# A fused two-block kernel: the end of a gated convolution, four up products and two gate sums rearranged

## The chip, the cores and the metric

One Trainium2 chip, one core of it. The metric is the device time of one execution in microseconds (us), the median of the runs. The engines are named as in the profile: PE is TensorE, PEld its weight load, DVE VectorE, ACT ScalarE, POOL GpSimd, SP SyncE.

## The reference, cut to what matters

The first block has two layers. In each, three branches (attention, pooling, neighbourhood attention) are projected, gated and summed, then an output product, and then a gated MLP with a short convolution:

```python
z = jnp.einsum('bsnc,ncd->bsnd', ys, w_branch[l])
gates = jax.nn.sigmoid(gl + b_gate[l]).reshape(B, S, N_BRANCH, D_MODEL)
merged = jnp.sum(gates * z, axis=2)
mix = jnp.einsum('bsd,de->bse', merged, w_out[l])
```

The second block begins with a gated convolution over 31 positions, with a layer norm, and an output product with a bias:

```python
u = h @ w_in + b_in
u = u[..., :D_MODEL] * jax.nn.sigmoid(u[..., D_MODEL:])
u = causal_dwconv(u, dw, dw_b)
u = layer_norm(u, ln_g, ln_b)
u = jax.nn.silu(u)
return u @ w_out + b_out
```

It then has two more gated MLPs and a dilated attention. There are 512 tokens and 1024 channels, all in float32.

## The kernel before, in words

**Products.** A weight product takes three TensorE passes over numbers split into a high and a low part (`whi`, `wlo`, and `hh`, `hl` or `yh`, `yl` or `uh`, `ul`). Weights come in chunks of 1 MB that SP loads into two slots `wraw` in a fixed order; `hi` on ACT (L817) makes `whi`, `lo` on DVE (L1278) makes `wlo`. `lo(c)` makes the low part of chunk c + 2, once PE is done with chunk c, and the load of chunk c waits until the low part of chunk c - 2 is made. PE accumulates in eight banks of 128 x 512 (`bank(0)` to `bank(7)`). All engines run programs written out in order, with semaphores between them.

**Up products (`ffn`, four of them).** `first_two` computes the first two chunks into banks 0 and 4, 1 and 5. Then a loop takes two chunks in a turn; the first goes to banks 2 and 3, the second to 0 and 1. Before each, PE waits for `conv_done`, the count of tiles that DVE has read out (L1476). In the first turn the first of these waits is for banks 0 and 4, which this chunk doesn't write.

**Gates and branches (`merge`, two layers, three branches).** For each branch n and half g there are two gate chunks (`gate_rows`, banks 6, 7 and 4, 5) and one branch chunk (`branch_rows`, banks 0 to 3). DVE adds the gate bias (L1725), ACT takes the sigmoid (L1138), DVE multiplies by the branch (L1732) and adds to `mg` (L1735), which a memset (L1718) clears first. Banks 4 and 5 are held by the attention and the pooling until the end of both, so PE waits for them (`y_lo`, `pool_lo`) ahead of the second gate chunk. At that point POOL starts `weight_sums`: four copies and four additions of 2.5 MB in DRAM, for later down products.

**End of the gated convolution.** The 31 taps of a channel tile are shared: DVE does `DVE_TAPS[t]` of them one after the other (L1798), PE the rest as 32 x 32 products (`partial_taps`, L2445), ACT copies the partial sums out, PE joins them (L2453), and DVE adds the two (L1773). For the last tile that is 11 taps on DVE and 20 on PE. Then the mean is taken by products with `meanm` (L2480, L2483), DVE subtracts it (L1848), ACT squares (L1198), and PE adds the squares up in products one column wide (L2491); POOL adds four tiles of squares into one (L691) so that PE takes five instead of eight. `keep_warm` (L1994) is a product of 512 columns whose result nobody reads. ACT takes the root, PE spreads it (L2495), DVE scales (L1859), ACT applies SiLU and splits, DVE makes the low part (L1284).

**Output product and hand-over.** `out_product` fills banks 4 to 7 (first half of the channels), then `last_two` banks 0 to 3. `hand_over` normalises, adds to the stream, and turns the rows for the next product. Only in the one after the gated convolution (h == 4) DVE first adds the bias `b_out` to each bank (L1325, L1336), and ACT waits for that before it squares.

Of the kernel before, what the change touches and what calls it, by code (L numbers as in the profile page):

```python
# [21 lines left out]
ALU = mybir.AluOpType  # L22
# [17 lines left out]
DVE_TAPS = (15, 15, 15, 15, 15, 15, 15, 11)  # L40
# [129 lines left out]
def build(nc, A, out):  # L170
    with ExitStack() as ctx:
# [67 lines left out]
        with ExitStack() as s:  # L239
# [3 lines left out]
            tapd = [sb(f"tapd{i}", 20 * 32, stack=s) for i in range(2)]  # L243
            part, usum, stack = sb("part", 8 * T, stack=s), sb("usum", T, stack=s), sb("stack", 32, stack=s)
# [9 lines left out]
        def bank(b, n=1):  # L254
# [18 lines left out]
        squared, summed, rooted, diagonal, spread, sq_added = (  # L273
            sem(n) for n in ("squared", "summed", "rooted", "diagonal", "spread", "sq_added"))
        gains_in, biased, half_squared, half_meaned, rest_squared, post_rooted = (
            sem(n) for n in ("gains_in", "biased", "half_squared", "half_meaned", "rest_squared", "post_rooted"))
# [360 lines left out]
        def _(pool):  # L637
# [46 lines left out]
            def add_squares():  # L684

                n = None
                for t in range(3, KT - 2):
                    pool.wait_ge(squared, t + 1)
                    if n:
                        ch.wait(n)  # L690
                    ins = gp.tensor_tensor(tile(sq, 2), tile(sq, 2), tile(sq, t), ALU.add)  # L691
                    if t < KT - 3:
                        n = ch.mark(ins)
                ins.then_inc(sq_added, 1)

# [78 lines left out]
            pool.dma_start(stack[:, :], A["c_stack"]).then_inc(stack_in, 16)  # L774
            pool.wait_ge(stack_in, 16)
# [11 lines left out]
            add_squares()  # L787
            pool.wait_ge(ln_scaled, KT)
            const(ub[:, 0:D], bass.AP(tensor=A["cm_b_out_2"].tensor, ap=[[0, P], [1, D]], offset=A["cm_b_out_2"].offset))
# [16 lines left out]
        def _(act):  # L806
# [45 lines left out]
            def half_squares(h, c, rows=(0, 1, 2, 3)):  # L852

                for b in rows:
                    if h == 4:
                        act.wait_ge(biased, b + 1)
                    elif h % 2:
# [9 lines left out]
            def post_root(h, c, b):  # L867

                if h == 4:
                    act.wait_ge(biased, 4 + b + 1)  # L870
                else:
                    act.wait_ge(*row_done(h, c, b))
# [194 lines left out]
            for l in range(2):  # L1067
# [78 lines left out]
                for g in range(2):  # L1146
                    for j in range(2):
                        gate(2, g, j)
                        if g == 1 and j == 0:
                            for t in range(4):  # L1150
                                act.wait_ge(merged, 9 * l + 5)
# [1488 lines left out]
```

## Time and profile before

| | |
|---|---|
| median of 3 runs | 3115.69 us (3114.3 to 3117.58) |
| the profiled execution's own time | 3114.26 us |
| its span, first to last instruction | 3112.5 us |
| PE busy | 98% |
| DVE, ACT, POOL busy | 59%, 41%, 6% |
| mean granted TensorE clock | 0.995 of 2.4 GHz |

Times of events are us from the start of the span. A number in brackets behind a row of the timeline is how long the engine was idle before it, and who ended that.

### The profile page before, as it was taken

How to read it: one execution, taken by the hardware profiler on the slowest of the kernel's cores; microseconds unless marked ns; L12 is line 12 of the kernel's file. 1: busy time of each engine (PE TensorE's matmuls, PEld its weight loads, DVE VectorE, ACT ScalarE, POOL GpSimd, SP SyncE). 2: the span in 40 equal slices, each digit the busy share in tenths (PEclk: the TensorE clock that was granted, in tenths of full speed). 3: DMA queues.
4: the chain of work that ended last, by engine and by line, in shares of the span. 5: the costliest groups of instructions: out<-in, count | busy, mean ns of one | idle time of the engine just before them, and what ended most of it. 6: DMA issues, size and time to landing. Idle time of an engine off the chain costs nothing.

```text
span 3112.5 us, 42337 instructions
## 1 busy us (share of the span) xinstructions
PE 3059.4 (98%) x16887; PEld 2530.3 (81%) x16887; DVE 1824.1 (59%) x2476; ACT 1263.0 (41%) x1786; POOL 178.9 (6%) x230
## 2 busy tenths in 40 slices
PE   7999999999999999999999989999999999999999
PEld 7767888888887688888888668888888988988887
DVE  4574446557755744556678866557743433465576
ACT  3563234335544622433464343336531221343355
POOL 2030000000012100000001110000000000000000
PEclk9999999999999999999999989999999999999999
DMA  6206853224532288322353157987432323233244
GB/s 174 71 28 220 193 141 108 95 94 143 167 89 79 74 238 199 98 95 95 106 183 97 54 186 182 302 192 210 144 110 95 109 88 102 95 110 100 94 133 158
DMA packets 298730, 408.95 MB, mean 131 GB/s; under 512 B 19796, under 2 KB 211324, under 8 KB 298332
## 3 DMA queue, kind: packets, MB, share of 16 engines
q1 hardware_dynamic: 251036, 306.75, 30.4%
q0 software_dynamic: 47552, 100.21, 13.6%
q8 instruction: 102, 1.67, 0.2%
q14 instruction: 40, 0.33, 0.0%
HBM read 400.54 MB, written 90.18 MB: 158 GB/s over the span
## 4 chain that ended last, share of the span: by engine, by line
PE 86%; DVE 8%; ACT 2%; DMA 1%; issue 1%; DVEq 0%; ACTq 0%; SPq 0%; POOL 0%; POOLq 0%
PE ps L1964 19%; PE ps L1966 19%; PE ps L1965 19%; PE ps L2119 4%; PE ps L2120 4%; PE ps L2121 4%; PE ps L2071 2%; PE ps L2073 2%; PE ps L2072 2%; PE ps L2524 1%; PE ps L2525 1%; PE ps L2526 1%; DVE t_wlo L1278 1%; DMA t_wraw<-in_w_in_dram 1%; DVE t_vb L1798 1%
## 5 line engine op out<-in xcount | busy, mean ns | idle before, releaser
L1964 PE MATMUL ps<-t_hh,t_whi 128*128 128x512 f32 (+1 forms) x2720 | 1015.0, 373 | 12.2 <-DVE t_accv L1476 5.1
L1966 PE MATMUL ps<-t_hh,t_wlo 128*128 128x512 f32 (+1 forms) x2720 | 1005.1, 370 | 0.0
L1965 PE MATMUL ps<-t_hl,t_whi 128*128 128x512 f32 (+1 forms) x2720 | 1004.9, 369 | 0.0
L1278 DVE TENSOR_TENSOR t_wlo<-t_wraw,t_whi 128x2048 fp32r<-128x2048 f32 x198 | 455.7, 2302 | 778.9 <-ACT t_whi L817 778.8
L817 ACT ACTIVATE t_whi<-t_wraw 128x2048 fp32r<-128x2048 f32 x198 | 379.3, 1916 | 1056.7 <-PE ps L1966 848.8
L1964 PEld LDWEIGHTS ps<-t_hh,t_whi 128*128 128x128 f32 x2720 | 513.3, 189 | 114.9 <-issue 16.8
L1965 PEld LDWEIGHTS ps<-t_hl,t_whi 128*128 128x128 f32 x2720 | 513.5, 189 | 87.0 <-issue 2.4
L1966 PEld LDWEIGHTS ps<-t_hh,t_wlo 128*128 128x128 f32 x2720 | 513.4, 189 | 86.8
L2119 PE MATMUL ps<-t_whi,t_ah 128*128 128x512 f32 x528 | 206.0, 390 | 0.0
L2121 PE MATMUL ps<-t_whi,t_al 128*128 128x512 f32 x528 | 205.4, 389 | 0.0
L2120 PE MATMUL ps<-t_wlo,t_ah 128*128 128x512 f32 x528 | 205.4, 389 | 0.0
L1295 DVE TENSOR_TENSOR t_wlo<-t_wraw,t_whi 128x1024 fp32r<-128x1024 f32 x148 | 181.1, 1224 | 19.7 <-ACT t_whi L842 19.1
L842 ACT ACTIVATE t_whi<-t_wraw 128x1024 fp32r<-128x1024 f32 x148 | 155.0, 1047 | 11.3 <-PE ps L2121 5.1
L840 ACT ACTIVATE t_ah<-t_mid 128x512 fp32r<-128x512 f32 x132 | 82.7, 626 | 118.9 <-PE ps L2121 105.4
L1293 DVE TENSOR_TENSOR t_al<-t_mid,t_ah 128x512 fp32r<-128x512 f32 x132 | 91.0, 689 | 67.0 <-ACT t_ah L840 67.0
L1476 DVE SCALAR_TENSOR_TENSOR t_accg<-ps,t_pvec,t_accg 128x511 f32<-128x511 f32 (+1 forms) x176 | 119.5, 742 | 0.0
L1476 DVE SCALAR_TENSOR_TENSOR t_accv<-ps,t_pvec,t_accv 128x511 f32<-128x511 f32 (+1 forms) x176 | 119.4, 742 | 0.0
L2119 PEld LDWEIGHTS ps<-t_whi,t_ah 128*128 128x128 f32 x528 | 99.1, 188 | 21.6 <-issue 1.2
L2121 PEld LDWEIGHTS ps<-t_whi,t_al 128*128 128x128 f32 x528 | 99.1, 188 | 20.5
L2120 PEld LDWEIGHTS ps<-t_wlo,t_ah 128*128 128x128 f32 x528 | 99.1, 188 | 20.3
L2524 PE MATMUL ps<-t_whi,t_hh 128*128 128x256 f32 x384 | 110.2, 287 | 0.0
L2526 PE MATMUL ps<-t_whi,t_hl 128*128 128x256 f32 x384 | 108.6, 283 | 0.0
(320 smaller groups left out, 4097.8 us busy)
## 6 DMA issues: line engine op xcount, KB each, us to landing
t_wraw<-in_w_in_dram SPq DMA_DIRECT2D x46, 1024.0 KB, 5.6
t_wraw<-in_w_up_dram SPq DMA_DIRECT2D x44, 1024.0 KB, 5.0
t_wraw<-in_ffn_w_in_dram SPq DMA_DIRECT2D x44, 1024.0 KB, 5.6
t_wraw<-sum_T SPq DMA_DIRECT2D x80, 512.0 KB, 4.0
sum_T<-in_w_down_dram POOLq DMA_DIRECT2D x12, 2560.0 KB, 32.1
sum_T<-in_ffn_w_out_dram POOLq DMA_DIRECT2D x12, 2560.0 KB, 30.6
t_wraw<-in_w_kv_dram SPq DMA_DIRECT2D x24, 1024.0 KB, 5.1
sum_T<-sum_T POOLq DMA_DIRECT2D x8, 2560.0 KB, 19.9
```

Source lines behind the costliest of these rows:

```text
L817: sc.activation(whi[slot][:, :], wraw[slot][:, :], ACT.Copy).then_inc(w_hi, 1)
L842: sc.activation(whi[slot][:, c0:c0 + 2 * T], wraw[slot][:, c0:c0 + 2 * T], ACT.Copy).then_inc(p_hi, 1)
L1278: v.tensor_tensor(wlo[slot][:, :], wraw[slot][:, :], whi[slot][:, :].bitcast(F32), ALU.subtract).then_inc(w_lo, 1)
L1295: v.tensor_tensor(wlo[slot][:, c0:c0 + 2 * T], wraw[slot][:, c0:c0 + 2 * T], whi[slot][:, c0:c0 + 2 * T].bitcast(F32), ALU.subtract).then_ ...
L1476: ins = v.scalar_tensor_tensor(out=tile(acc, m)[:, o0:o1], in0=from_bank(s, m)[:, i0:i1], scalar=col(cw, r), in1=tile(acc, m)[:, o0:o1], o ...
L1964: te.matmul(out, wh, xh, start=first, stop=False)
L1965: te.matmul(out, wh, xl, start=False, stop=False)
L1966: return te.matmul(out, wl, xh, start=False, stop=last)
L2119: te.matmul(o, lh, wh, start=opens and k == 0, stop=False, skip_group_check=n >= 20)
L2120: te.matmul(o, lh, wl, start=False, stop=False, skip_group_check=n >= 20)
L2121: ins = te.matmul(o, ll, wh, start=False, stop=closes and k == 1, skip_group_check=n >= 20)
L2524: te.matmul(o, xh, wh, start=k == 0, stop=False)
```

## The change

- `DVE_TAPS[7]` goes from 11 to 7, so PE does 24 taps of the last tile.
- POOL no longer adds squares; PE takes all eight tiles of them. All `keep_warm` products go.
- The bias `b_out` is loaded early into a buffer of its own (`brow`), and PE puts it into the eight banks of the output product itself, as `ident` times `brow`, an accumulation that the product then goes on with (`bias_in`, `opened`). Two banks are filled behind the mean, two behind the squares, three behind the spread, and the last between the two chunks of the first half. DVE's eight additions and ACT's waits for them go.
- The second `lo` of this stage, `lo(c + 7)`, moves from behind the centring into the scaling, behind its sixth tile.
- In `ffn` the third and fourth chunk are written out ahead of the loop; the third waits for its weights alone.
- In `merge` the second gate chunk of the first branch goes to banks 0 and 1 and ahead of the wait for `y_lo`; its branch chunk takes tiles 2 and 3 first, and waits ahead of tile 0 until DVE has read the gate. The first branch's product is written straight into `mg`, so the memset and one addition per half go; DVE's loop over two branches is written out.

```diff
-DVE_TAPS = (15, 15, 15, 15, 15, 15, 15, 11)
+DVE_TAPS = (15, 15, 15, 15, 15, 15, 15, 7)
...
+            const(brow[:, :], bass.AP(tensor=A["cm_b_out_2"].tensor, ap=[[0, P], [1, D]], offset=A["cm_b_out_2"].offset))
...
-            add_squares()
             pool.wait_ge(ln_scaled, KT)
-            const(ub[:, 0:D], ...)
...
-                if h == 4:
-                    dve.wait_ge(tables, 16 * 9)
-                    dve.wait_ge(w_used, c + 1)
-                    for b in range(4):
-                        v.tensor_tensor(bank(4 + b), bank(4 + b), ub[:, 0:T], ALU.add).then_inc(biased, 1)
...
-                cleared = ch.mark(v.memset(mg[:, :], 0.0))
...
+                    out = gates[:, :] if n else tile(mg, 4 * g, 4)
+                    v.tensor_tensor(out, gates[:, :], bank(0, 4), ALU.mult).then_inc(drained, 1)
...
-            lo(c + 7)
...
+                if t == 5:
+                    lo(c + 7)
...
+            def bias_in(*banks):
+
+                for b in banks:
+                    te.matmul(bank(b), ident, brow[:, 0:T] if b >= 4 else brow[:, T:D], start=True, stop=False)
...
                 first_two(c, f"pre{2 * f + 1}")
-                with pe.Fori(1, FT // 2) as i:
+                pe.wait_ge(w_lo, c + 3)
+                rows_out(c, (hh, hl), bank0=2).then_inc(w_used, 1)
+                pe.wait_ge(w_lo, c + 4)
+                pe.wait_ge(conv_done, 4 + 2 * m0 + 4)
+                rows_out(c + 1, (hh, hl), bank0=0).then_inc(w_used, 1)
+                with pe.Fori(2, FT // 2) as i:
...
+                    for t in tiles:
+                        if t == 0 and tiles[0]:
+                            pe.wait_ge(drained, 2 + d + 2)
...
+                gate_rows(0, 0, 1, 0)
                 pe.wait_ge(y_lo, PAIRS[f"A{l}"] + 4)
+                branch_rows(0, 0, (2, 3, 0, 1))
                 pe.wait_ge(pool_lo, 4 * l + 4)
-                gate_rows(0, 0, 1)
-                branch_rows(0, 0)
...
-            for t in (0, 1, KT - 2, KT - 1, 2):
-                if t in (KT - 2, 2):
-                    keep_warm()
-                pe.wait_ge(*((sq_added, 1) if t == 2 else (squared, t + 1)))
+            pe.wait_ge(tables, 16 * 9)
+            bias_in(5, 1)
+            for t in range(KT):
+                pe.wait_ge(squared, t + 1)
...
-            keep_warm(1)
+            bias_in(4, 0)
             pe.wait_ge(diagonal, 1)
             te.matmul(bank(3), meanm, std, start=True, stop=True).then_inc(spread, 1)
-            keep_warm(2)
+            pe.wait_ge(centred, KT)
+            pe.wait_ge(rooted, 1)
+            bias_in(7, 2, 6)
             pe.wait_ge(drained, 2 + d + 8)
-            pe.wait_ge(h_lo, SPLIT["ln"] + 1)
-            out_product(2, (uh, ul), "ln", None)
+
+            def last_bias():
+
+                pe.wait_ge(ln_scaled, KT)
+                bias_in(3)
+
+            out_product(2, (uh, ul), "ln", None, last_bias)
```

## Rows read from the trace of the kernel before

**Rows 1.** The page, busy time of each engine and its share of the span.

```profile
PE 3059.4 (98%) x16887; PEld 2530.3 (81%) x16887; DVE 1824.1 (59%) x2476; ACT 1263.0 (41%) x1786; POOL 178.9 (6%) x230
```

**Rows 2.** The waits, of PE: us in total, times, longest.

```profile
PE ps L1964 <- DVE t_accv L1476: 5.1, 4, 1.3
PE ps L2483 <- DVE t_small L1777: 3.7, 2, 3.3
...
PE ps L1964 <- DVE t_yl L1453: 2.8, 2, 1.4
```

**Rows 3.** The timeline of DVE, the last taps: start, us, instruction.

```profile
1786.58 12.00 DVE L1798 SCALAR_TENSOR_TENSOR t_vb<-t_ub,t_pvec,t_vb 128x512 f32<-128x512 f32 x18
1798.50 0.68 DVE L1773 TENSOR_TENSOR t_vb<-t_vb,ps 128x512 f32<-128x512 f32 x1
1799.22 0.75 DVE L1798 SCALAR_TENSOR_TENSOR t_vb<-t_ub,t_pvec,t_vb 128x512 f32<-128x512 f32 x1
...
1800.00 0.69 DVE L1773 TENSOR_TENSOR t_vb<-t_vb,ps 128x512 f32<-128x512 f32 x1
```

**Rows 4.** The timeline of PE, from the mean to the output product (two passes per product).

```profile
1799.36 1.12 PE L2483 MATMUL ps<-t_vb,t_base 128*128 128x512 f32 x2 [3.28 <-DVE t_small L1777]
1800.87 2.08 PE L2483 MATMUL ps<-t_vb,t_base 128*128 128x512 f32 x2 [0.39 <-DVE t_small L1777]
1804.39 3.57 PE L2491 MATMUL ps<-t_base,t_sq 128*128 128x1 f32 x16 [1.44 <-ACT t_sq L1198]
...
1816.35 2.05 PE L1994 MATMUL ps<-t_base 128*128 128x512 f32 x2
1818.20 1.92 PE L2495 MATMUL ps<-t_gain,t_base 128*128 128x512 f32 x2
1819.91 2.52 PE L1994 MATMUL ps<-t_base 128*128 128x512 f32 x4
1823.22 0.47 PE L2071 MATMUL ps<-t_whi,t_uh 128*128 128x512 f32 x1 [0.80 <-DVE t_ul L1284]
```

**Rows 5.** Windows there: us; busy PE, PEld, DVE, ACT, POOL; PEclk; DMA share; GB/s.

```profile
1797.28:1800.69 3.41, 1.12 (x2) 0.30 (x2) 3.33 (x6) 0.00 (x0) 0.00 (x0) 1.00 0.00 0
...
1807.52:1810.93 3.41, 3.41 (x12) 2.38 (x11) 3.41 (x2) 1.00 (x2) 3.16 (x2) 0.50 0.00 0
...
1817.76:1821.17 3.41, 3.41 (x5) 1.58 (x5) 1.17 (x3) 0.63 (x2) 0.00 (x0) 0.50 0.28 109
```

**Rows 6.** Windows from the output product to the third up chunk: first layer, gated convolution.

```profile
441.62:513.70 72.08, 70.51 (x418) 62.47 (x416) 45.07 (x60) 33.54 (x55) 1.14 (x2) 1.00 0.29 93
...
1823.22:1903.68 80.46, 73.92 (x417) 65.11 (x417) 48.30 (x66) 37.93 (x63) 7.89 (x8) 0.96 0.74 231
```

**Rows 7.** The timeline of PE, products two columns wide at full clock, layer 0.

```profile
149.83 1.84 PE L2313 MATMUL ps<-t_base,t_gain 128*128 128x2 f32 x16
```

**Rows 8.** Groups of DVE from 1847 to 1880: busy, mean ns, idle before.

```profile
L1278 DVE TENSOR_TENSOR t_wlo<-t_wraw,t_whi 128x2048 fp32r<-128x2048 f32 x3 | 6.9, 2292 | 9.0 <-ACT t_whi L817 9.0
...
L1336 DVE TENSOR_TENSOR ps<-ps,t_ub 128x512 f32<-128x512 f32 x4 | 2.8, 690 | 0.0
```

**Rows 9.** Windows of PE in the first MLP: us, PE busy (x), PEclk, DMA share, GB/s.

```profile
514.00:604.00 90.00, 90.00 (x398) 1.00 0.30 100
```

**Rows 10.** The timeline at the first gates of layer 0: PE, then DVE, SP and ACT.

```profile
255.26 0.50 PE L1964 MATMUL ps<-t_hh,t_whi 128*128 128x512 f32 x1 [1.42 <-DVE t_yl L1453]
...
270.71 1.40 DVE L1725 TENSOR_SCALAR t_gates<-ps,t_pvec 128x512 f32<-128x512 f32 x2
...
261.80 0.37 SPq L570 DMA_DIRECT2D t_wraw<-in_w_in_dram  x1
...
282.04 1.92 ACT L817 ACTIVATE t_whi<-t_wraw 128x2048 fp32r<-128x2048 f32 x1 [8.83 <-DMA t_wraw<-in_w_in_dram]
```

**Rows 11.** The timeline of PE at the third up chunk of the first MLP.

```profile
512.14 0.28 PE L1966 MATMUL ps<-t_hh,t_wlo 128*128 128x256 f32 x1
513.70 0.50 PE L1964 MATMUL ps<-t_hh,t_whi 128*128 128x512 f32 x1 [1.28 <-DVE t_accv L1476]
```

More of the change, by code:

```diff
@@ L242, in build @@
             ub, vb = sb("ub", KT * UW, stack=s), sb("vb", KT * T, stack=s)
-            tapd = [sb(f"tapd{i}", 20 * 32, stack=s) for i in range(2)]
-            part, usum, stack = sb("part", 8 * T, stack=s), sb("usum", T, stack=s), sb("stack", 32, stack=s)
+            tapd = [sb(f"tapd{i}", 24 * 32, stack=s) for i in range(2)]
+            part, usum, stack, brow = (sb(n, w, stack=s) for n, w in (("part", 8 * T), ("usum", T), ("stack", 32), ("brow", D)))
         with ExitStack() as s:
@@ L272, in build @@
         init_in, init_turn, init_out, stored = sem("init_in"), sem("init_turn"), sem("init_out"), sem("stored")
[L273 to L276, printed above, removed]
+        squared, summed, rooted, diagonal, spread = (
+            sem(n) for n in ("squared", "summed", "rooted", "diagonal", "spread"))
+        gains_in, half_squared, half_meaned, rest_squared, post_rooted = (
+            sem(n) for n in ("gains_in", "half_squared", "half_meaned", "rest_squared", "post_rooted"))
         x_new, row_squared, pre_rooted, rows_ready, rows_turned = (
@@ L682, in by_tile @@
                 return ap.rearrange("p i n -> i p n")
[L684 to L694, printed above, removed]
             for l in range(2):
@@ L1722, in gate @@
                 def gate(n, g, j, l=l, c=c):
[L1723 removed]
+                    lo(c + 6 * n + 3 * g + j)
+                    b0 = 0 if (n, g, j) == (0, 0, 1) else 6 - 2 * j
                     for m in range(2):
[L1725 to L1726 removed]
+                        ins = v.tensor_scalar(tile(gates, 2 * j + m), bank(b0 + m),
+                                              col("b_gate", 8 * n + 24 * l + 4 * g + 2 * j + m), None, ALU.add)
                     ins.then_inc(drained, 1)
                 def weighted_sum(n, g, l=l, c=c, d=d):
[L1730 to L1738 removed]
+                    lo(c + 6 * n + 3 * g + 2)
+                    dve.wait_ge(gate_sig, 12 * l + 4 * n + 2 * g + 2)
+                    out = gates[:, :] if n else tile(mg, 4 * g, 4)
+                    v.tensor_tensor(out, gates[:, :], bank(0, 4), ALU.mult).then_inc(drained, 1)
+                    dve.wait_ge(drained, 2 + d + 6 * n + 3 * g + 3)
+                    if n:
+                        v.tensor_tensor(tile(mg, 4 * g, 4), tile(mg, 4 * g, 4), gates[:, :], ALU.add).then_inc(merged, 1)
+                        dve.wait_ge(merged, 7 * l + 2 * n + g - 1)
+                for n in range(2):
                     for g in range(2):
@@ L1989, in rows_out @@
                 return row_tile(c, bufs, 1, bank(b0 + 1))
-            def keep_warm(n=1):
-                for _ in range(n):
-                    te.matmul(bank(5), meanm, base[:, 0:T], start=True, stop=True)
+            def bias_in(*banks):
+                for b in banks:
+                    te.matmul(bank(b), ident, brow[:, 0:T] if b >= 4 else brow[:, T:D], start=True, stop=False)
             def turn_row(name, b, turned_in=None):
@@ L2063, in first_two, with token_tile @@
                 rows_half(c + 1, (hh, hl), 1, 1).then_inc(w_used, 1)
-            def token_tile(c, bufs, b, half, k0, k1, last, ks=None):
+            def token_tile(c, bufs, b, half, k0, k1, last, ks=None, opened=False):
                 for k in (ks or range(k0, k1)):
@@ L2070, in token_tile @@
                     o = bank(4 * (1 - half) + b)
-                    te.matmul(o, xh, wh, start=k == 0, stop=False)
+                    te.matmul(o, xh, wh, start=k == 0 and not opened, stop=False)
                     te.matmul(o, xh, wl, start=False, stop=False)
@@ L2074, in token_tile, with tokens_mix @@
                 return ins
-            def tokens_mix(c, half, bufs, k0, k1, last, ready=None):
+            def tokens_mix(c, half, bufs, k0, k1, last, ready=None, opened=False):
                 pe.wait_ge(w_lo, c + 1)
```

58 lines of the change are left out of this document (16 added, 42 removed).

## The prediction

> **What bounds the kernel now.** First the page: PE is busy for 98% of the span [rows 1], so a part of the change can only pay where PE stands idle, runs at the lower clock, or does less. Then the waits of PE [rows 2]: three of them lie where the change works. PE waits four times, 5.1 us in all, for the readout of the first up tiles; twice, 2.8 us, for the last low part of the attention; and twice, 3.7 us, for DVE's last taps. Then, for the end of the convolution, the timelines of DVE and PE and windows with the granted clock [rows 3 to 5]. The reader is to see a chain: DVE's taps end late, PE idles for 3.28 us, the clock falls to 0.50 at 1800.69, and it is back only at 1821.17, although PE is busy in each window between. What fills those windows is mostly products one column wide. So this stretch costs twice, by idle time and by the clock. Last, windows from the first product of an output product to the third up chunk: 72.08 us in the first layer, 80.46 behind the convolution [rows 6].
>
> **The last taps.** From 1786.58 to 1798.50 DVE does 18 taps, two tiles in alternation, 0.66 us each; one behind another of the same tile takes 0.78 (1799.22 to 1800.00) [rows 3]. Four taps fewer: three of the 18 and the one at 1799.22. Two of those left, and the addition, now stand behind their own tile, 3 x 0.12 more. Before the first addition: 11.92 - 3 x 0.66 + 0.36 = 10.3, so it starts at 1796.9; the second addition follows at once, and the signal that PE got at 1800.87 [rows 4] comes at 1798.45, 2.4 us earlier. PE takes 16 products of 32 x 32 more; no row here prices them, but PE idled 3.28 us just behind [rows 4], so a cost up to that is covered; I take about 1 us. The idle shrinks to about 1 us.
>
> **The mean.** A product of 512 columns took 1.12 us with its tail at the full clock and 2.08 at the half [rows 4]. With PE nearly always busy I take the clock as full here. The centring, which started 0.1 us behind 1800.87 + 2.08, then starts at 1799.8, 3.2 earlier.
>
> **Squares and first biases.** One product of 512 columns holds PE for 1.71 us at the half clock (1818.20 to 1819.91), so 0.86 at the full. `bias_in(5, 1)` is 1.7 us, 1799.5 to 1801.2, and lies beside the 1.40 us that centring and squaring take (1.44 of idle at 1804.39). It delays nothing. Each tile of squares is eight passes: 3.57/16 = 0.22 us a pass with the tail, so 1.7 us a tile at the half clock; at the full clock the two-column products took 1.70/16 = 0.11 a pass [rows 7], 0.87 a tile. Eight tiles: 7.0 us at full, 13.7 at half. Before, five tiles and two `keep_warm` and the wait for POOL took 1804.39 to 1816.35 = 12.0. Which clock? In the window 1807.52:1810.93 PE was busy throughout, more than half of it with a full-width product, and the clock stayed at 0.50 [rows 5]; so I take it to fall while the squares run, at 1805 as a middle. By then 4.4 tiles are done; 3.6 at 1.71 end at 1811.2, and the root comes at 1811.5 against 1816.5. The Trainium skill, TensorE: Matmul & The Clock Gate, Part 1, says that an idle PE brings the lower clock and sustained activity the full one. Read plainly, a PE without a gap would keep 2.4 GHz; the row just named doesn't bear that out. That reading is rival A.
>
> **Spread and the other biases.** `bias_in(4, 0)` is queued ahead of the spread: 3.4 us at the half clock, while the diagonal needed 1.7 (1816.5 to 1818.2). So the spread waits 1.7 to 2 us for the biases; at the full clock (1.7) it waits for nothing. Spread ends and DVE scales at 1811.4 + 3.4 + 1.95 = 1816.7 against 1820.15 (3.4 earlier). `bias_in(7, 2, 6)` is 2.6 to 5.1 us beside the 2.9 us to the first low part (1820.15 to 1823.07); the products of full width in a row raise the clock again, as they did at 1821.17, so I take it as covered. The output product starts at 1819.6 instead of 1823.2: **3.6 us**. Bounds: full clock throughout gives 1814.3 (8.9); the clock down already at the mean gives 1826.2 (minus 3.0), with 13.7 for squares, 3.7 and 3.4 and 5.1 for biases in line.
>
> **The moved `lo`.** It puts one low part, 2.3 us [rows 8], into DVE's scaling, behind tile 6 of 8. PE takes 10.9 us for the first chunk (48 products of 90/398 = 0.226) [rows 9], then needs this low part at about 13.9 us behind the start of scaling; it is there at 9.2 (six scalings and four low parts of 0.69, then 2.3). The tiles behind it are needed one per 2.7 us from 13.9 on and come from 10.7 on: covered by 3 us or more. Behind it in SP's queue is the load of the fourth output chunk, issued at 1826 instead of 1814, and behind the eighth scaled tile POOL starts its 10 MB of copies, at 1828. The load is needed on chip by about 1842.6. In layer 0 a load amid such copies took 261.80 to 282.04 = 20.2 us [rows 10]; so the bound is 1846, some 3 us late; with a head start of 3 us I take nothing. POOL itself loses three additions and one load.
>
> **The hand-over.** Eight additions of 0.69 us on DVE go (four at L1336, as many at L1325), 5.5 us [rows 8], and ACT's waits for them. The first layer has the same stage without them: 80.46 - 72.08 = 8.4 us, of which PE idle is 6.54 - 1.57 = 5.0 and the clock (0.96 against 1.00) the rest [rows 6]. Added: `bias_in(3)`, in line, 0.9. Sum **7.5 us**. Bounds: 3.5 if up weights loaded amid POOL's copies come late (in this stage the DMA share is 0.74 against 0.29), 8.4 if the bias were free.
>
> **Third up chunk.** Its weights are ready ahead of it. The gap is 513.70 - 512.14 - 0.12 (half of 0.226 and a little, for a product of 256 columns) = 1.44 us [rows 11], and DVE had all of this turn's reads done 4 us before the fourth chunk wants them. Four times: **5.8 us**; bounds 5.1 [rows 2] and nothing, if a later wait took it back; no other wait of PE in these loops is in the list.
>
> **Gates.** PE no longer idles at 255.26: 1.42 and a short start, 1.6. The branch chunk then runs two tiles, 24 x 0.226 = 5.4 us, but the gate is read 272.1 - 266.1 = 6.0 us behind the chunk's end [rows 10], so a new wait of 0.6: net 1.0 for each layer. Dropped DVE work (memset 3.5, four additions of 2.3) hides beside PE and gains nothing itself, but lets the next load start 1.7 us earlier. Behind, in layer 0, PE meets a chunk that came late from DRAM (the wait ended at 282.04); if its landing doesn't move, that layer gains nothing. **2.0 us**; bounds 0.5 and 3.
>
> **The sum.** 3.6 + 7.5 + 5.8 + 2.0 = 18.9. Against the execution's own time, 3114.26 (span 3112.5 and 1.8 around it): 3095.4. The median of the runs is 1.4 above that execution: **3096.8**.
>
> **The rivals.** A, the squares hold the full clock: the tail gives 8.9, the time is 3091.5. For it: PE has no long gap left. Against: [rows 5]. B, the clock is already down at the mean: the tail loses 3.0, 3103.4. For it: joins with small gaps stand ahead of it. Against: before the 3.28 us gap it held at 1.00. C, the hand-over waits for up weights behind POOL's copies, which now stand nearer to it: 4 us less, 3100.8. For it: 20.2 us a load. E, the bank moves don't do what they say, since the next wait on DVE or DRAM takes their place: 7.8 less, 3104.6. D, slower: the fourth output chunk, now issued only 2 us ahead of POOL's copies, lands with them instead of in 20 us. DVE's part, and PE, hand-over and all, wait for it. From a landing at 1842.6 + 18.9 = 1861.5 on, the kernel is slower than before; landing after 50 us, 1876, gives 33 lost, 3130. Against it: each load seen amid copies came in about 20. The Trainium skill, DMA: Bandwidth & Descriptors, Queues, rings and completion order, says that an engine takes turns between queues packet by packet; by it a load shares, and is not held to the end of the copies, which agrees with 20.2 us and keeps D small.
>
> **How the numbers follow.** Forecast 0.50; A 0.14; B 0.12; C 0.12; E 0.08; D 0.04. What is left of a fixed difference is told from none from 0.2%, 6.2 us, on. A to E alone all lie beyond it, but B, C and E together would give 3112: I leave 0.04 for such a sum, taken from theirs. So faster 0.92, same 0.04, slower 0.04. The range goes from 3091 (A) to 3105 (E).
>
> **What would show it.** The signal behind the last tap near 1798.4, and no idle of PE over 1.5 us ahead of the mean; one fall of the clock during the squares and none in the hand-over; first output product near 1819.6 and 71.5 us from there to the third up chunk; no wait for L1476 at the up products; at the gates a wait for L1725 of 0.6 in place of 1.4. Wrong would be: a DMA as the one who ends a wait of L817 in the hand-over, or the biases in line for over 6 us.

## The result, and the profile after

The changed kernel takes 3096.47 us (median of 4 runs, 3095.39 to 3098.06), the kernel before on the same chip 3114.99 (4 runs, 3112.68 to 3117.58). The ratio is 0.9941 with a 95% interval of 0.9929 to 0.9952: 18.5 us faster, against 18.9 forecast. The profiled execution has a span of 3095.0 us and took 3096.8 us.

Below, the page of after, busy time by engine, against [rows 1]. PE still is the bound; it is busy as long as before, and idles less.

```profile
PE 3058.1 (99%) x16949; PEld 2529.8 (82%) x16949; DVE 1799.1 (58%) x2458; ACT 1263.1 (41%) x1786; POOL 173.4 (6%) x227
```

The waits of PE after, against [rows 2]: us in total, times, longest. Four waits for the readout (`t_accv`) are one, 3.7 us for the last taps (`t_small`) are 0.8, and a gate's wait (`t_gates`) is new in place of the one for `t_yl`.

```profile
PE ps L1933 <- DVE t_accv L1444: 1.3, 1, 1.3
...
PE ps L1933 <- DVE t_gates L1693: 0.9, 3, 0.4
PE ps L2459 <- DVE t_small L1746: 0.8, 1, 0.8
```

The end of the convolution after, timelines of DVE (against [rows 3]) and of PE (against [rows 4]): start, us, instruction, idle before.

```profile
1782.20 10.26 DVE L1767 SCALAR_TENSOR_TENSOR t_vb<-t_ub,t_pvec,t_vb 128x512 f32<-128x512 f32 x15
1792.50 0.69 DVE L1742 TENSOR_TENSOR t_vb<-t_vb,ps 128x512 f32<-128x512 f32 x1
...
1794.05 0.06 DVE L1746 MEMSET t_small<- 128x1 f32 x1
```

```profile
1793.37 1.98 PE L2459 MATMUL ps<-t_vb,t_base 128*128 128x512 f32 x4 [0.84 <-DVE t_small L1746]
1795.19 1.88 PE L1963 MATMUL ps<-t_brow,t_base 128*128 128x512 f32 x4
1796.91 9.29 PE L2467 MATMUL ps<-t_base,t_sq 128*128 128x1 f32 x64
1806.05 3.76 PE L1963 MATMUL ps<-t_brow,t_base 128*128 128x512 f32 x4
1809.61 1.92 PE L2471 MATMUL ps<-t_gain,t_base 128*128 128x512 f32 x2
1811.31 3.05 PE L1963 MATMUL ps<-t_brow,t_base 128*128 128x512 f32 x6
```

PE now works without a gap from the mean to the output product (1814.63, behind 0.27 us of idle), and the mean's product is at full clock. Windows of after: us; busy PE, PEld, DVE, ACT, POOL; PEclk; DMA share; GB/s. The first runs from the mean over `bias_in(5, 1)` into the squares, at full clock; the second is the rest of the squares, at half; the third is `bias_in(4, 0)`. The last is the stage from the output product to the third up chunk (which starts at 1886.29), against [rows 6].

```profile
1794.00:1801.60 7.60, 7.60 (x51) 5.92 (x50) 6.27 (x10) 4.82 (x8) 0.00 (x0) 1.00 0.01 3
1801.70:1806.00 4.30, 4.30 (x22) 4.30 (x22) 0.76 (x1) 0.00 (x0) 0.00 (x0) 0.50 0.54 154
1806.06:1809.60 3.54, 3.54 (x5) 1.48 (x6) 1.05 (x5) 1.55 (x2) 0.00 (x0) 0.50 0.26 102
...
1814.63:1886.43 71.80, 71.50 (x419) 63.13 (x420) 43.84 (x58) 36.63 (x62) 7.37 (x7) 1.00 0.79 253
```

The clock falls once, at 1801.69 in the squares, and is full again from 1811.93 on.

**Where the 17.5 us of span came from.** Positions of the same product in both traces give: gates of layer 0 1.5; third up chunk of the first MLP 1.5; gates of layer 1 0.5; second MLP 1.6; tail of the convolution 3.9; hand-over behind it 7.4; third MLP 0.0; fourth MLP 1.5. That is 17.9, less 0.5 by which this execution began later. The same code was profiled a second time ("The changed kernel again", below), and there the same positions give 21.5 (parts and sum are rounded alone):

| | forecast | after | after, second profile |
|---|---|---|---|
| tail | 3.6 | 3.9 | 5.4 |
| hand-over | 7.5 | 7.4 | 7.3 |
| third up chunk, four times | 5.8 | 4.6 | 6.0 |
| gates, two layers | 2.0 | 2.0 | 2.8 |
| sum | 18.9 | 17.9 | 21.5 |

So a part read from one profile can be off by 1.5 us.

The third MLP's zero is the place of the first profile that differs most from the forecast. Its third chunk has no wait any more, but four chunks on PE waits 1.28 us. Timelines of POOL, SP, ACT and PE there: an addition between DRAM tensors is under way from 1900.49 to 1930.83; the load of up weights issued at 1905.24 beside it lands 19.1 us later; ACT, which had waited for it for 8.53 us, splits it late, and PE stops. PE's wait names the readout, which stands behind that split in ACT's queue.

```profile
1900.49 1.92 POOL L674 DMA_DIRECT2D sum_T<-in_ffn_w_out_dram  x1 [25.79 <-issue]
1905.24 0.37 SPq L570 DMA_DIRECT2D t_wraw<-in_ffn_w_in_dram  x1
1924.35 1.92 ACT L804 ACTIVATE t_whi<-t_wraw 128x2048 fp32r<-128x2048 f32 x1 [8.53 <-DMA t_wraw<-in_ffn_w_in_dram]
1931.28 0.50 PE L1933 MATMUL ps<-t_hh,t_whi 128*128 128x512 f32 x1 [1.28 <-DVE t_accv L1444]
```

### The profile page after: what moved, and what is told of

Same layout as the page of the kernel before. It is cut to its first block, busy times and chain, and to the rows that moved or that the text cites. A ratio compares the mean times of both kernels' runs of the same rounds, so it can differ in the third digit from the quotient of the medians.

```text
span 3095.0 us, 42330 instructions
## 1 busy us (share of the span) xinstructions
PE 3058.1 (99%) x16949; PEld 2529.8 (82%) x16949; DVE 1799.1 (58%) x2458; ACT 1263.1 (41%) x1786; POOL 173.4 (6%) x227
## 4 chain that ended last, share of the span: by engine, by line
PE 85%; DVE 8%; DMA 4%; ACT 2%; issue 1%; DVEq 0%; ACTq 0%; SPq 0%; POOL 0%; POOLq 0%
PE ps L1933 18%; PE ps L1935 18%; PE ps L1934 18%; PE ps L2088 4%; PE ps L2090 4%; PE ps L2089 4%; DMA t_wraw<-in_w_in_dram 3%; PE ps L2040 2%; PE ps L2042 2%; PE ps L2041 2%; DVE t_wlo L1260 1%; PE ps L2507 1%; PE ps L2508 1%; PE ps L2509 1%; ACT t_whi L804 1%; PE ps L2149 1%
## 5 line engine op out<-in xcount | busy, mean ns | idle before, releaser
L804 ACT ACTIVATE t_whi<-t_wraw 128x2048 fp32r<-128x2048 f32 x198 | 379.3, 1916 | 1053.5 <-PE ps L1935 834.9
L2089 PEld LDWEIGHTS ps<-t_wlo,t_ah 128*128 128x128 f32 x528 | 99.1, 188 | 20.5
L2508 PE MATMUL ps<-t_wlo,t_hh 128*128 128x256 f32 x384 | 108.6, 283 | 0.0
```

Source lines behind the costliest of these rows:

```text
L804: sc.activation(whi[slot][:, :], wraw[slot][:, :], ACT.Copy).then_inc(w_hi, 1)
L2089: te.matmul(o, lh, wl, start=False, stop=False, skip_group_check=n >= 20)
```

## Experiments

Two theories of the gain stand against each other. Mine: four parts with a price each (tail 3.6, hand-over 7.5, third up chunk 5.8, gates 2.0), independent of one another. The rival: PE waits taken out are given back at the next late load, so that parts don't add up. Every ratio is to the kernel before on the same chip. Three distances read from each trace do most of the work, in us:

| kernel | A: second MLP's first up product to output product | B: from there to the 73rd up product behind the last turned rows | C: the next 912 up products |
|---|---|---|---|
| before | 519.48 | 73.27 | 203.22 |
| after | 513.99 | 65.90 | 203.21 |
| after, second profile | 512.62 | 65.94 | 201.81 |
| up products only | 517.88 | 73.27 | 203.75 |
| gates only | 518.07 | 73.27 | 203.44 |
| bias by DVE | 513.72 | 75.87 | 202.75 |
| 11 taps | 515.69 | 65.92 | 202.01 |
| biases between squares | 515.95 | 65.97 | 203.43 |
| wide squares | 510.52 | 67.53 | 203.98 |
| wide, filled | 510.52 | 65.93 | 206.17 |
| POOL's squares | 514.05 | 65.93 | 204.03 |
| sums early | 518.69 | 65.90 | 201.63 |
| sums beside the down products | 543.70 | 65.92 | 201.63 |
| sums spread | 510.54 | 75.61 | 201.63 |

A holds the second MLP's third chunk (1.5 of the 519.48 - 517.88 = 1.6 is that part) and the tail. Its spread between executions is as large: 1.4 between the two profiles of after, and 1.4 between before and the kernel with the gates only, whose edit touches nothing in A; in both pairs the clock's low stretch in the tail differs. C without any wait is 201.63; what is above it is waits, with up to 0.3 us behind each in which PE is slower than its usual pace. One profile stands behind each row.

**The up products alone.** The kernel before, with

```diff
-                with pe.Fori(1, FT // 2) as i:
+                pe.wait_ge(w_lo, c + 3)
+                rows_out(c, (hh, hl), bank0=2).then_inc(w_used, 1)
+                pe.wait_ge(w_lo, c + 4)
+                pe.wait_ge(conv_done, 4 + 2 * m0 + 4)
+                rows_out(c + 1, (hh, hl), bank0=0).then_inc(w_used, 1)
+                with pe.Fori(2, FT // 2) as i:
```

> The kernel before, with only the third and fourth chunk of the four up projections written out and the third put into the banks that need no drain. By the prediction's step for the up products (four waits of 1.28 to 1.45 us removed) it is 5.8 us faster than before. The rival is what the changed kernel's trace shows at its third up projection: there the gain of 1.44 us was lost again, to a wait of 1.28 us that ends with a late load of up weights. If that wait is the price of the earlier hand-over (GpSimd's copies between DRAM tensors then lie nearer the loop), it is absent here and all four places give 1.4 us; if it is the price of the earlier third chunk alone, it is here too, and the sum is 4.4 us.

Measured: 3109.99 against 3114.55, ratio 0.9986 (0.9977 to 0.9995), 4.6 us faster. The four waits are gone, and in the third MLP two came in their place (0.38 us, and the row below); its C is 203.75 against 203.22. So the third MLP gave nothing here either, with the hand-over unmoved: the earlier hand-over isn't needed for the late load. By positions the other three places gave 1.5 each and the third MLP -0.5, 4.1 us in all; the rest of this profile's 4.8 is chance at the gates and the tail. The runs' interval (1.6 to 7.2 us) holds 5.8 as well as 4.4, so it is the trace, of one execution, that speaks for the second theory.

```profile
2052.74 0.50 PE L1964 MATMUL ps<-t_hh,t_whi 128*128 128x512 f32 x1 [1.13 <-DVE t_accv L1476]
```

**The gates alone.** The kernel before, with the gates' part of the diff.

> The kernel before, with only the gates' part: the second gate chunk to banks 0 and 1, the branch product's tiles in the order 2, 3, 0, 1, and the first branch stored in place of cleared and added. The prediction gave 1.0 us a layer, 2.0 in all. The trace of the changed kernel reads 1.5 us in the first layer and 0.5 us in the second, which is the same sum: if the two parts are independent of the rest, this kernel reads 2.0 us faster than before. If later loads take the gain back once the up products don't use it, it reads 0 to 1 us.

Measured: 3112.99 against 3114.55, ratio 0.9995 (0.9986 to 1.0004), 1.6 us, which by itself isn't told from nothing. The trace shows both halves of the step. The wait of 1.42 us is gone and one of 0.36 is there, as in after; and later in layer 0 stands a wait of 1.09 for a chunk that came late, where the kernel before had 0.44 and 0.29, after 0.30, and the second profile of after nothing.

```profile
271.14 0.50 PE L1965 MATMUL ps<-t_yh,t_whi 128*128 128x512 f32 x1 [0.36 <-DVE t_gates L1725]
310.65 0.47 PE L1965 MATMUL ps<-t_hh,t_whi 128*128 128x512 f32 x1 [1.09 <-DVE t_gates L1725]
```

By the position of the same product the step nets 0.8 us in layer 0 and 0.9 in layer 1, in this kernel and in both profiles of after: 1.5 for the wait removed, 0.6 to 0.7 for the new one, as PE also loses 0.1 to 0.3 us behind each wait. Late chunks (0 to 1.4 us by execution, before's 0.73 among them) move that: after's 1.5 in layer 0 has 0.7 from them, and its 0.5 in layer 1 has lost 0.4 to one.

**The bias by DVE.** The changed kernel, with eight additions of `brow` in DVE's `half_mix` and `bias_rest`, as before, and

```diff
-            bias_in(5, 1)
...
-            bias_in(4, 0)
...
-            bias_in(7, 2, 6)
...
-            out_product(2, (uh, ul), "ln", None, last_bias)
+            out_product(2, (uh, ul), "ln", None)
```

> The changed kernel, but the output bias of the convolution is added to the product by VectorE again, in eight additions, and the eight products that open TensorE's banks with it are gone. By the prediction's step for the hand-over this gives back 7.5 us (the trace of after reads 7.4 us less between output product and third chunk), less what TensorE saves: two of the bias products (3.05 and 2.28 us in the trace of after) lie between the spread and the output product, though VectorE's scale runs beside them. So 7.4 us slower than after. If the hand-over were bound by the load of the weights and not by VectorE's additions, it is under 3 us slower. The copies of GpSimd and the load of the up weights keep their order; if the wait of 1.28 us of the third up projection goes away when the hand-over is long again, 1.3 us of it comes back, and the net is 6.1 us slower.

Measured: ratio 0.9975 (0.9965 to 0.9985) against after's 0.9941, 10.6 us slower than after, 3 more than expected. B is 75.87: 7.37 of the difference is what before has over after, the additions; the other 2.60 go with the clock. PE now waits 1.44, 1.48 and 3.10 us in the tail (first fence), the clock that fell at 1801.81 is full only from 1822.29, and the output product's first 6.1 us run at half (second fence: a window, columns as above).

```profile
1795.16 1.98 PE L2478 MATMUL ps<-t_vb,t_base 128*128 128x512 f32 x4 [0.84 <-DVE t_small L1765]
1798.59 10.91 PE L2484 MATMUL ps<-t_base,t_sq 128*128 128x1 f32 x64 [1.44 <-ACT t_sq L1185]
1810.97 2.07 PE L2487 MATMUL ps<-t_gain,t_base 128*128 128x512 f32 x2 [1.48 <-DVE t_gain L1841]
...
1816.15 0.76 PE L2059 MATMUL ps<-t_whi,t_uh 128*128 128x512 f32 x1 [3.10 <-DVE t_ul L1271]
```

```profile
1815.40:1822.20 6.80, 6.05 (x14) 4.78 (x15) 6.57 (x8) 6.56 (x10) 0.00 (x0) 0.50 0.00 0
```

A is 513.72 against after's 513.99 (and 512.62), so in these traces the biases cost the tail nothing or 1.1 us. What they put in front of the spread (3.76 us) they gave back elsewhere: without them the squares took 10.91 us in place of 9.29, and PE waited 1.48 us for the spread.

**11 taps of the last tile.** The changed kernel, with

```diff
-DVE_TAPS = (15, 15, 15, 15, 15, 15, 15, 7)
+DVE_TAPS = (15, 15, 15, 15, 15, 15, 15, 11)
...
+            tap(7, 9)
             add_joined(6, True)
+            tap(7, 10)
             add_joined(7, True)
```

> The changed kernel, but VectorE computes 11 taps of the last tile in place of 7, and TensorE 20 in place of 24. Four more taps at 0.67 us each (12.00 us for 18 in the trace of before) put the last addition 2.7 us later, and all behind it: 2.7 us slower than after by the prediction's step. If TensorE's join of the last tile set the end and not VectorE's taps, or if the later mean only uses up slack of the squares, it is under 1 us slower.

Measured: 3099.99 against 3114.55, ratio 0.9960 (0.9946 to 0.9973), 5 runs from 3096.8 to 3106.5: about 5 us slower than after by the ratios, whose intervals overlap. In the trace, taken of the fastest of the five, A is 1.7 more than in the first profile of after and 3.1 more than in the second; the 18 taps take 12.00 us, as before. PE idles 3.34 us in front of the mean, and the mean's products already run at half clock (3.68 us in place of 1.98). DVE's taps set the end, as the step said; the 2.7 us expected lie between the two readings of A.

```profile
1793.87 3.68 PE L2461 MATMUL ps<-t_vb,t_base 128*128 128x512 f32 x4 [3.34 <-DVE t_small L1746]
```

**Biases between the squares.** The changed kernel, with

```diff
+                if t in (2, 5):
+                    bias_in(4 if t == 2 else 0)
             ins.then_inc(summed, 1)
-            bias_in(4, 0)
```

> The changed kernel, but the two bias products of banks 4 and 0 stand between the narrow products of the squares (behind the third and the sixth tile) and not behind them, in front of the spread. In the trace of after the clock falls to its half at 1801.69, within the squares; the 20 narrow products left (40 passes) take 0.213 us a pass in place of 0.112, and the two bias products 3.76 us in place of 1.88, with the spread behind them. If wide products between the narrow ones hold the clock, squares and biases end 3.7 us earlier, and the scale, then behind the spread at full clock and DVE's 1.1 us, about 2.5 us earlier: 2.5 us faster than after. If the clock falls within the squares as before, the root comes later by what the biases take there, the spread has no bias in front of it any more, and the sum is within 0.5 us of after.

Measured: ratio 0.9944 (0.9930 to 0.9957), the same as after. A wide product behind the first 12 narrow ones (24 passes) didn't hold the clock: it fell at 1801.49, 0.2 us from where it fell in after, and the second wide one came at 1804.82, at half clock. The clock stayed low for 13.7 us in place of 10.2, and PE had 1.48 us of idle in front of the spread. A is 2.0 more than in the first profile of after; the second theory of the expectation holds, and its 0.5 us was too little. (The expectation counts 40 passes left behind the fall in after; there were 21.)

**Wide squares.** The changed kernel, with

```diff
-                for b in range(4):
-                    at = t * T + b * P
-                    ins = te.matmul(bank(6)[:, b:b + 1], sq[:, at:at + P], meanm[:, 0:1], start=t == b == 0, stop=t == KT - 1 and b == 3)
+                ins = te.matmul(bank(6), meanm, tile(sq, t), start=t == 0, stop=t == KT - 1)
...
-            te.matmul(bank(3), meanm, std, start=True, stop=True).then_inc(spread, 1)
```

and the root and its reciprocal over 512 columns, by which DVE scales.

> The changed kernel, but the sum of squares is made by eight full-width products (the matrix of means by a tile of squares, 512 columns) into one bank; ScalarE takes the root of the bank's 512 columns, VectorE its reciprocal of 128x512, and the spread product is gone. From rows: eight such products at 0.86 us at full clock put the last square at 1804.0, 2.2 us before after's; root of 512 columns 0.8 us, reciprocal 3.35 us (two such in the trace of before), no diagonal (1.1 us) and no spread (1.9 us at half clock), and the scale reads SBUF. Sum: the scale starts at 1808.2 in place of 1811.56, 3.4 us faster than after, if full-width products hold the clock. If the clock falls as with the narrow products, the eight take up to 1.7 us each in the slow part, the last square is at about 1807, and it is 0.5 us faster to 0.5 us slower.

Measured: ratio 0.9933 (0.9920 to 0.9947), which overlaps after's. A is 510.52, 3.5 less than in the first profile of after and 2.1 less than in the second: the clock stays full through squares and biases, and eight full-width products (16 passes) take 7.03 us, for 9.29 of the 64 narrow passes. But the biases end at 1809.5, PE idles 2.93 us behind them, the clock falls at 1812.78 for 3.4 us, and B is 1.6 more.

```profile
1798.17 7.03 PE L2460 MATMUL ps<-t_sq,t_base 128*128 128x512 f32 x16
1805.04 4.45 PE L1958 MATMUL ps<-t_brow,t_base 128*128 128x512 f32 x10
...
1812.42 0.47 PE L2035 MATMUL ps<-t_whi,t_uh 128*128 128x512 f32 x1 [2.93 <-DVE t_ul L1266]
```

**Sums early.** The changed kernel, with POOL's `weight_sums(2)` (four copies, four additions, all between DRAM tensors) issued in parts in its loop over the convolution's tiles in place of behind `gains(4)`, and `weight_sums(3)` behind `const(dmask[:, :], A["c_dmask"])`.

> The changed kernel, but the weight sums of the third MLP (four copies between DRAM tensors and four additions to them, GpSimd's queue) are issued during the convolution, where SyncE's queue loads almost nothing, and those of the fourth MLP behind the third MLP's end. In the trace of after the loads of the up weights take 14 to 20 us each beside them (5 to 7 without), and one that landed at 1924.32 costs TensorE the wait of 1.28 us at 1931.28. If these sums are what makes the load late, the third up projection has no wait for a load: 1.3 us faster than after in a profile that had the wait, with the loads down to 5 to 8 us there, and less spread between executions. If the wait is of the written-out loop's own period (slots come free too late), it stays with loads of 6 us. Slower would be a sum that the third MLP then waits for, or a late last addition that delays the gains of the hand-over.

Measured: ratio 1.0054 (1.0041 to 1.0068), 35 us slower than after. Of the 29.3 us that the profile's span is longer, nearly all comes from two waits that the expectation didn't name: POOL, held up by its own additions, made PE's tap matrices late by 2.66 us, which also lowered the clock; and a move of `t_vD` through DRAM, in SP's queue beside the sums, took 25 us and stopped PE for 23.83 us in the last attention.

```profile
1752.79 0.72 PE L2422 MATMUL ps<-t_ub,t_tapd 32*32 32x512 f32 x16 [2.66 <-POOL t_tapd L756]
...
2365.39 0.55 PE L2559 MATMUL ps<-t_yD,t_vD 128*128 128x128 f32 x1 [23.83 <-issue]
```

What it was made for it shows: in the third up projection there is no wait (C is 201.63), and from 1890 to 2000 the loads land in a median of 5.0 us (first fence), against 14.4 in the second profile of after (second fence): KB each, median us to landing.

```profile
t_wraw<-in_ffn_w_in_dram SPq DMA_DIRECT2D x11, 1024.0 KB, 5.0
```

```profile
sum_T<-in_ffn_w_out_dram POOLq DMA_DIRECT2D x5, 2560.0 KB, 30.7
t_wraw<-in_ffn_w_in_dram SPq DMA_DIRECT2D x9, 1024.0 KB, 14.4
```

**POOL's squares.** The changed kernel, with `add_squares` back in POOL's queue and PE taking five tiles of squares (0, 1, 6, 7 and the sum in 2) in place of eight.

> The changed kernel, but the squares' part is as before: GpSimd adds the squares of the third to sixth tile, TensorE takes five tiles in place of eight, with two bias products in front of the seventh and the third tile where products without a use stood. It prices TensorE's taking of all eight. In the trace of before the root is at 1816.5, 17.1 us behind the first product of the means; in that of after 12.9 us behind it, but the clock was at its half in more of the first. By the prediction's step (3.6 us for the whole tail, of which 2.4 are the taps') this part is worth 1.2 us: 1.2 us slower than after. If GpSimd's chain of additions set the root before, it is 3 to 4 us slower.

Measured: ratio 0.9945 (0.9932 to 0.9959), against 0.9941. A is 514.05: 0.1 more than the first profile of after, 1.4 more than the second. PE waits for ACT twice (1.53 and 0.61 us), the clock falls at 1801.21. So the eight tiles by PE are worth 0 to 1.4 us. With 1.7 to 3.1 for the taps, that leaves 1 to 2 us of the tail's 3.9 to 5.4 for what no run priced alone: the moved `lo`, the `keep_warm` products gone, and what the clock does by execution.

**Wide squares, filled.** The wide squares, with

```diff
             bias_in(7, 2, 6)
+            for _ in range(3):
+                te.matmul(bank(3), ident, brow[:, T:D], start=True, stop=True)
```

> The kernel of the wide squares, with three products without a use (into bank 3, which is free there) behind the last bias product of its row, so that TensorE works on until the output product. In the trace of the wide squares the output product started 3.5 us earlier than after's, each set against the second MLP's position, but TensorE had waited 2.93 us for it, the clock was at its half from 1812.78 to 1816.19, and of the 3.5 us 1.8 were left at the third chunk. If the idle time made the clock fall, the three products (0.86 us each) keep it up: 1.6 us faster than the wide squares, 3.4 us faster than after. If the clock falls all the same, it is within 0.5 us of the wide squares.

Measured: 3093.54 (5 runs) against 3095.62 of the changed kernel on the same chip; ratios 0.9934 (0.9921 to 0.9948) and 0.9943 (0.9929 to 0.9956), which overlap; nor is it told from the wide squares without filling (0.9933). In the trace the expectation holds to the tenth: A 510.52, B 65.93, the clock doesn't fall at all, 3.5 us less than the first profile of after (2.1 less than the second). And C is 206.17: PE waits 1.80 and 2.11 us for late loads. What the tail gained over after's first profile was given back, 3.0 of 3.5, by 1931.

```profile
1906.81 0.50 PE L1928 MATMUL ps<-t_hh,t_whi 128*128 128x512 f32 x1 [1.80 <-DVE t_accv L1444]
...
1930.97 0.50 PE L1928 MATMUL ps<-t_hh,t_whi 128*128 128x512 f32 x1 [2.11 <-DVE t_accv L1444]
```

**Sums beside the down products.** The wide, filled kernel, with this in front of `weight_sums(3)`, and the like at the end of the second MLP's up projection for `weight_sums(2)`:

```diff
+            pool.wait_ge(conv_done, 4 + 2 * FT * 2 + 2 * FT)
             weight_sums(3)
```

> The kernel just above, and the weight sums of the third MLP are issued at the end of the second MLP's up projection, those of the fourth at the end of the third's, so that they run beside the down products and not beside an up projection or a hand-over. Moved into the convolution they took the load wait out of the third up projection (1.3 to 1.7 us in four of the traces), but held up GpSimd's own work there (2.7 us) and a transfer of the last attention (23.8 us). If the down products' loads, which are small and land in 4 to 5 us, have the slack for it, this is 1.3 us faster than the kernel above. If they have not, TensorE waits at the ring of pieces: 19 us landings in place of 4 would show as waits of several us, and it is 5 to 30 us slower.

Measured: 3173.42, ratio 1.0195 (1.0180 to 1.0210), 78 us slower than after. The second theory, and more than it said: the waits of PE name 33 at the down products, and one of 15.3 us for rows that their late end delayed.

```profile
PE ps L2086 <- DVE t_wlo L1280: 36.8, 33, 3.2
...
PE ps L1971 <- DVE t_accv L1341: 15.3, 1, 15.3
PE ps L1931 <- DVE t_wlo L1288: 8.5, 2, 5.7
```

**The changed kernel again.**

> The changed kernel itself, unaltered, for a second profile and a ratio beside the two kernels of this call. If the wait of 1.28 us in the third up projection belongs to this order of work and not to one execution, it is here again, between 1 and 1.7 us, with a load that lands 18 to 20 us after its issue; if it is chance, it is gone or elsewhere. The ratio to before is 0.994 again.

Measured: 3095.62 against 3114.23, ratio 0.9943 (0.9929 to 0.9956). The wait in the third MLP is gone: C is 201.81, with a load that again took 19.2 us but was issued 3.7 us earlier (PE stood 2.2 us earlier). And the clock, which fell at 1801.63, was back after 6.8 us and not 10.2, so A is 1.4 less. Same code, 2.8 us of difference at two places, and a span of 3091.4; it is the fastest of the five executions.

**Sums spread.** The wide, filled kernel; of `weight_sums(2)` the copies go behind the convolution's first tile, the additions behind its fourth and sixth and its end (two); `weight_sums(3)` waits for about nine chunks of the third up projection.

> The wide squares with filled idle time, and the weight sums moved so that neither GpSimd's own work nor a transfer stands behind them: of the third MLP's, the four copies are issued behind the first tile of the convolution, the first addition behind its fourth tile, the second behind its sixth, the other two at its end; the fourth MLP's wait for the ninth chunk or so of the third up projection, where they stood in time in the trace of after (1969). In the profile of the kernel it starts from, the output product began 3.3 us before after's and the third up projection then lost 1.80 and 2.11 us to late loads. If the sums between DRAM tensors are the whole of that lateness, the loads there land in 5 to 8 us, both waits are gone, and the span is 3.9 us less than 3094.7, 3090.8; the median 2 to 4 us below 3093.5. The rival is that the waits move: loads of the convolution then take 20 us in place of 5, and a wait of 1 to 3 us there or at the output product's third and fourth chunk takes the place of those removed.

Measured: 3102.22 against 3116.13, ratio 0.9954 (0.9940 to 0.9967), some 4 us slower than after, with intervals that just overlap. The loads are quick (5.1 us from 1900 to 1960) and C is 201.63, so the waits were the sums'. The wait moved to a place that neither theory named: the additions at the convolution's end held POOL until 1827.21, `gains(4)` behind them was issued 5 us later than in after and landed beside the last one at 1848.6 and 1850.4 in place of 1827.2 and 1830.0. DVE waited for the gains until 1850.47 where it had started at 1843.43, and PE 7.55 us (timelines of DVE and PE); the clock was at its half from 1853.82 to 1864.06. B is 9.7 us more by both.

```profile
1850.47 0.17 DVE L1307 TENSOR_SCALAR t_small<-t_small 128x4 f32<-128x4 f32 x1 [11.22 <-DMA t_gain<-in_ffn_pre_g_dram]
```

```profile
1858.76 0.69 PE L1971 MATMUL ps<-t_base,t_vb 128*128 128x128 f32 x2 [7.55 <-DVE t_vb L1341]
```

## Why the prediction was right, and where its terms were off

**The last taps** (2.4 us): right. The prediction's times are those of the trace before; PE's position ahead of the tail is 4.66 us earlier in after, so each time below has 4.66 added. The 15 taps ended 10.3 us behind their start, as worked out, and PE idled 0.84 us where 1 was taken.

**The tail** (3.6 us; measured 3.9, and 5.4 in the second profile): the intermediate times fit too. The fall of the clock was put at 1805 and came at 1806.35; root 1811.5, came 1810.9; scale 1816.7, came 1816.2; output product 1819.6, came 1819.3. That the clock fell in the squares was read from one window of the trace before, and 1805 was a middle without a reason of its own, so the fit to 1.4 us is partly luck. The prediction says that mostly products one column wide filled the low stretch before: by count they do (40 passes of some 52), by time they don't (8.5 of 20.5 us), and in the first of its windows PE was busy for 2.08 of 3.41 us only. What narrow products do was shown only by the wide squares. Rival A (full clock throughout the squares) is refuted by after's window of 4.30 us with PE busy for all of it at 0.50, and again by the biases between the squares. Rival B needed the clock down at the mean; the kernel with 11 taps shows it there, with 3.34 us of idle ahead. In these traces PE stayed at 2.4 GHz through full-width products without a gap (wide, filled), and fell to 1.2 GHz in a narrow row without one. The Trainium skill, TensorE: Matmul & The Clock Gate, HAM oscillation, blames waits of PE for a lower clock; the wide squares agree, where 2.93 us of idle cost 1.6 us more behind it and three products without a use took that away. The fall in a narrow row without a gap is not in that rule.

**The hand-over** (7.5 us; measured 7.37, with B at 65.90 to 65.97 in eight traces). The step counted DVE's additions and `bias_in(3)`. What the biases do for the clock ahead of the output product the tail's step took as covered, without a price; the bias by DVE gives it, 2.6 us more lost. Rival C is refuted: B stays the same at a DMA share of 0.79.

**Third up chunk** (5.8 us; measured 4.1 alone, 4.6 in the profile of after, 6.0 in the second): a term that holds only when no load comes late. The step multiplied 1.44 by four, with the argument that no other wait of PE in these loops is in the list. Each place gives 1.5. But in the third MLP the loads land 6 to 20 us after their issue beside POOL's sums (5.0 without them); the wait for the readout had left them slack, and with it removed late loads took 0.2 to 2.4 us back, by execution, and 4.5 where the stage began earliest. That is rival E at one place of four. C shows it: from 201.8 to 206.2 with the sums beside it, and 201.63 in all three kernels without them. In the kernel before, C holds the 1.44 us of the wait removed, and 0.15 more.

**Gates** (2.0 us; measured 2.0, and 2.8 in the second profile, with a new wait of 0.36 and 0.28 in place of 0.6): the mechanism is right and nets 1.7; the 0.3 on top, and the second profile's 1.1, is the chance of a late chunk.

**Rival D** (the fourth output chunk lands with POOL's copies) is refuted: issued at 1820.82, 3.2 us ahead of the first copy, it landed at 1825.90. The head start was enough for all of it. The Trainium skill, DMA: Bandwidth & Descriptors, Queues, rings and completion order, has an engine take turns between queues; the 19.1 us of a load beside a sum of 30 us, against 5.0 alone, agree: it is slowed, and not held to the sum's end.

**The signs.** The signal behind the last tap came at 1798.7 for 1798.4, the stage behind the output product took 71.7 us for 71.5, and no DMA ended a wait of ACT's split (L817 before, L804 after) in the hand-over. One sign failed: there is still a wait for the readout at the up products, the 1.28 us above.

In all, the profile gives 3.9 + 7.4 + 4.6 + 2.0 = 17.9 for 18.9, the second 21.5, and the medians 18.5 and 18.6. The mechanisms are those of the prediction; a sum right to 0.4 us, where single terms move by 0.8 to 1.5 us between executions, is luck in its last digit. One of the prediction's sums is wrong, without effect on the forecast: rivals B, C and E together give 3115.2 and not 3112. What stays open: why the same code's clock comes back after 6.8 us once and 10.2 another time, and what the moved `lo` and the `keep_warm` products were worth. No version is faster than the changed kernel beyond doubt; the wide, filled one is the nearest, and its 3.5 us would count only with the third MLP's loads freed, for which none of the three places tried for the sums was free.

## What to carry to other kernels

A wait that is removed pays in full only if the load behind it has slack: compare the time from issue to landing with the time to its use, not just the list of waits, which names none as long as an earlier wait covers it. A queue that carries long transfers holds up all that stands behind them, so moving them needs the list of what is queued behind at the new place: of three places tried here, none was free. And work that seems free on PE may carry the clock: price its removal with the products that follow it.

## What the runs showed of the hardware beyond that

- In one row of 64, back to back, passes one column wide took 0.112 us each at full clock and 0.213 at half. Sixteen full-width passes took 7.03 us at full clock. The clock fell within the narrow row in each of the seven traces of kernels derived from the changed one that have it, between 1801.2 and 1805.2, in five of them with no gap of PE between the mean and that point; in none of the four whose squares are wide did it fall there.
- One load of 1 MB takes 5.0 us alone, and 19.1 beside an addition of 2.5 MB between DRAM tensors (6 to 20 over the third up projection); a second such addition is issued on POOL's queue only when the first has landed (1872.78, then 1900.49 with 25.79 us ahead of it), though nothing in the code waits between them.
